# The bias of a pooling mixer: as a one-row product on TensorE, or as a spread row added on VectorE

## The reference

```python
x = layer_norm(ALPHA * x + moe, ln_g[0, 1], ln_b[0, 1])      # end of the first layer
f = pool_mixer(x, pool_w, pool_b, pool_scale)                # (pooled(x) @ w + b) * scale, in 4 groups of 256 columns
x = layer_norm(ALPHA * x + f, ln_g[1, 0], ln_b[1, 0])        # then the router's logits of the second layer
```

## Time and profile before

| | us |
|---|---|
| median of 3 runs | 3657.47 |
| lowest, highest | 3655.7, 3662.36 |
| the profiled execution's own time | 3655.02 |
| its span in the trace | 3653.2 |
| TensorE busy in the span | 3035.5 (83%) |
| VectorE busy in the span | 1163.9 (32%) |
| ScalarE busy in the span | 775.7 (21%) |
| mean granted TensorE clock | 0.919 |

### The profile page before, as it was taken

The page is one execution under the profiler, slowest core; times in us unless marked ns, Lnnn a source line. Parts: engine busy times, 40 slices in busy tenths (PEclk is TensorE's granted clock), DMA queues, the critical chain, the costliest instruction groups (busy, mean ns, idle before and its releaser), DMA issues. The chain is left out here.

```text
span 3653.2 us, 41438 instructions
## 1 busy us (share of the span) xinstructions
PE 3035.5 (83%) x16259; PEld 1793.2 (49%) x16259; DVE 1163.9 (32%) x1986; ACT 775.7 (21%) x1306; POOL 354.6 (10%) x370
## 2 busy tenths in 40 slices
PE   6999879897999999988999997787687577876770
PEld 3455478445888878774555544332222453322220
DVE  1046668223111113321555535211111462111116
ACT  3011222113121212324333311100000331010002
POOL 0000045112000000110000000111110001111102
PEclk9999989898999999999999998899899678998995
DMA  7401000402111114212000022799998437999984
GB/s 264 148 18 34 17 1 1 150 29 87 46 47 51 46 64 143 87 62 90 17 7 6 1 85 113 295 419 419 419 416 335 163 129 293 419 420 420 417 362 197
DMA packets 187340, 615.44 MB, mean 168 GB/s; under 512 B 39241, under 2 KB 101776, under 8 KB 131746
## 3 DMA queue, kind: packets, MB, share of 16 engines
q1 hardware_dynamic: 168738, 579.55, 40.7%
q0 software_dynamic: 18432, 33.60, 2.5%
HBM read 592.08 MB, written 54.53 MB: 177 GB/s over the span
## 5 line engine op out<-in xcount | busy, mean ns | idle before, releaser
L2525 PE MATMUL psum<-moe_ring,hreg 128*32 128x512 f32 x3072 | 387.4, 663 | 144.9 <-DMA moe_ring<-in_moe_w 143.2
L2525 PEld LDWEIGHTS psum<-moe_ring,hreg 128*32 128x32 f32 x3072 | 116.8, 121 | 411.6 <-issue 324.4
L2610 DVE TENSOR_TENSOR ex_hb<-ex_sil,psum 128x256 f32<-128x256 f32 x64 | 26.9, 421 | 639.2 <-ACT ex_sil L2582 639.2
L1084 PE MATMUL psum<-h_hi,gu_hi 128*128 128x512 f32 x704 | 217.7, 391 | 9.2 <-DVE gu_lo L1125 9.2
L1084 PE MATMUL psum<-h_lo,gu_hi 128*128 128x512 f32 x704 | 217.5, 390 | 0.0
L1084 PE MATMUL psum<-h_hi,gu_lo 128*128 128x512 f32 x704 | 217.2, 390 | 0.0
L2557 PE MATMUL psum<-moe_ring,hreg 128*32 128x512 f32 x1728 | 193.7, 601 | 16.2 <-issue 11.3
L501 PE MATMUL psum<-h,pj_w 128*128 128x512 f32 x448 | 194.1, 592 | 0.8 <-ACTq L530 0.8
L2582 ACT ACTIVATE ex_sil<-psum 128x256 f32<-128x256 f32 x64 | 24.5, 383 | 628.9 <-PE psum L2525 628.9
L1084 PEld LDWEIGHTS psum<-h_hi,gu_hi 128*128 128x128 f32 x704 | 132.6, 188 | 36.9 <-issue 9.4
L1084 PEld LDWEIGHTS psum<-h_lo,gu_hi 128*128 128x128 f32 x704 | 132.7, 189 | 27.6
(11 more groups left out here) (498 smaller groups left out, 4819.2 us busy)
## 6 DMA issues: line engine op xcount, KB each, us to landing
moe_ring<-in_moe_w SPq DMA_DIRECT2D x288, 1024.0 KB, 21.1
x<-in_moe_w SPq DMA_DIRECT2D x96, 1024.0 KB, 22.4
draw<-in_w_down SPq DMA_DIRECT2D x44, 512.0 KB, 3.7
XF<-in_w_ada SPq DMA_DIRECT2D x16, 1024.0 KB, 5.8
x<-xrow SPq DMA_DIRECT2D x24, 512.0 KB, 10.4
gu_raw<-in_w_gate SPq DMA_DIRECT2D x22, 512.0 KB, 3.9
gu_raw<-in_w_up SPq DMA_DIRECT2D x22, 512.0 KB, 3.9
mo_dft<-in_dft SPq DMA_DIRECT2D x8, 1024.0 KB, 4.9
```

Of the source, the lines that this page charges most:

```text
L1084: last = pe.matmul(ps[4 * s + 2 * j + h][:, :], w[j][:, k, :], x[:, k, h * 512:(h + 1) * 512], start=k == 0 and n == 0, stop=k == KD - 1 a ...
L2525: last = pe.matmul(ps[i][r, :], xT[i][:, k, r], ring[n % RING][:, j, kk * 512:(kk + 1) * 512], start=k == 0, stop=k == KD - 1)
L2610: dve.tensor_tensor(hb[i][:, :], sil[q % 2][:, :], ps[i][:, DE:2 * DE], ALU.mult).then_inc(hbd, 1)
```

## The change

The rows `c` and `pb` become tiles of 128 equal rows, loaded with a broadcast in the transfer. Their product and sum in `weights()` run on 128 partitions. `residual(t)` gets a drain and an add of `c` behind the product with `ga`. In `mix` the one-row product goes, each group of two products starts its own quarter of PSUM anew, and the wait for `one` goes with the constant.

```diff
-        c, pb, one = sb("c", [1, D]), sb("pb", [1, D]), sb("one", [1, P])
+        c, pb = sb("c", [P, D]), sb("pb", [P, D])
...
-                sp.dma_start(c[:, :], A["ln_b_2"][0, 1:2, :]).then_inc(row_in, 16)
-                sp.dma_start(pb[:, :], A["pool_b_2"]).then_inc(row_in, 16)
+                sp.dma_start(c[:, :], A["ln_b_2"][0, 1:2, :].to_broadcast([P, D])).then_inc(row_in, 16)
+                sp.dma_start(pb[:, :], A["pool_b_2"].to_broadcast([P, D])).then_inc(row_in, 16)
...
-                pool.memset(eps[:, :], LN_EPS)
-                pool.memset(one[:, :], 1.0).then_inc(ones, 1)
+                pool.memset(eps[:, :], LN_EPS).then_inc(ones, 1)
...
-                    dve.tensor_tensor(pb[:, :], pb[:, :], sc[0:1, :], ALU.mult)
+                    dve.tensor_tensor(pb[:, :], pb[:, :], sc[:, :], ALU.mult)
...
                     dve.tensor_tensor(X[:, t, :], n_[t % NN], ga[:, :], ALU.mult).then_inc(scaled, 1)
+                    dve.drain()
+                    dve.tensor_tensor(X[:, t, :], X[:, t, :], c[:, :], ALU.add)
...
-                        pe.wait_ge(ones, 1)
...
-                        pe.matmul(ps[2 + h][:, :], one[:, :], c[:, h * 512:(h + 1) * 512], start=True, stop=False)
                         for g in (2 * h, 2 * h + 1):
                             for k in range(2):
                                 last = pe.matmul(ps[2 + h][:, (g % 2) * 256:(g % 2 + 1) * 256], PM[t % 2][:, 2 * g + k, :], w[:, g, k, :],
-                                                 start=False, stop=g % 2 == 1 and k == 1)
+                                                 start=k == 0, stop=k == 1)
```

## The result

| | before | after |
|---|---|---|
| median, us | 3658.51 (4 runs) | 3635.81 (4 runs) |
| lowest, highest | 3655.7, 3662.36 | 3630.52, 3636.53 |
| the profiled execution's span | 3653.2 | 3628.7 |
| mean granted TensorE clock | 0.919 | 0.921 |

The changed kernel takes 0.9934 of the time of the kernel before, with a 95% interval of 0.9917 to 0.9951. That is faster by 22.7 us at the medians, clearly outside 0.2%. Later sessions agree: medians of 3658.5, 3660.2 and 3658.8 for the kernel before, and of 3635.3 for the changed one in the last of them. The profiled execution of the changed kernel, at 3630.52 us, is the fastest of its four, 5.3 us under their median. So its trace shows a somewhat better case than the median.

The account below looks back on a forecast made before the run. TensorE was taken to bound the stage between the experts. Tile intervals 23.7 us less, last mix 2.1 less, broadcasts 2.5 more: 23.3 less, or 20.3 with 3 us for a remaining clock fall, giving 3637 us; range 3630 to 3647.

Parts of the forecast that it names:

- TensorE sets the pace of the stage: Stage between the experts, about 2844 to 2999 us: TensorE bounds it at 12.14 us a tile; gains reach the end one to one.
- 19.7 us come off TensorE: Sixteen one-row products in the mixes go: 13 at 1.05 us and three at 2.0 us; 2.10 us a steady tile.
- The add costs only what VectorE's pace costs: VectorE, each tile: the new add takes 1.30 us, raising its work to 10.28 us, ahead of TensorE's 10.04.
- a chain over two tiles: One tile followed through the engines to the total of the tile after next: 20.9 us for two tiles, 10.5 a tile.
- The broadcasts cost 2.5 us: Start of the stage, SP's queue: 1.04 MB of spread rows ahead of tile loads 1 to 3 cost 2.5 us in the open.
- The 3.7 us more: Spread-row transfer: the Trainium skill prices 1 MB at 6.15 us, which would make the result 3.7 us later.
- Most falls of the clock go: TensorE in the mixes: 9.9 us went to 1.2 GHz; without the one-row product most falls go, 3 us left in.
- The 3 us that I left in: Allowance, out of 9.9 us, for the clock fall behind tile 1, whose idle 1.27 us ahead of the mix stays.
- (a): TensorE's clock still falls as before: about 9 of the 9.9 us stay, time 3643; chance 0.23.
- (b): VectorE's add lies wholly in the open and the clock falls stay: 6.8 us gained, time 3650.7; chance 0.10.
- (c): No gain: the wait reappears behind the barrier or the first expert transfers, time 3657; chance 0.06.
- (d): TensorE, starved just enough, stays at 1.2 GHz for the whole stage: 18 us slower, 3675; chance 0.05.

Follow-up runs that it names:

- the loop cut: Changed kernel without VectorE's add, ScalarE's second norm of the previous tile moved ahead of the copy of the pooled tile: 3636.10 us, tiles of 9.97 us.
- the swap: ScalarE's second norm of the previous tile put ahead of the pooled tile's copy, against the changed kernel: 3640.16 us with VectorE's add kept, 3636.10 without.
- the one with zeros: Kernel with spread rows and a 128-row product, with ones in the first row and zeros in 127 instead of 1/128 throughout: 3644.05 us.
- the add on top: Kernel before with the two rows spread, one-row product kept, plus the 128x1024 add on VectorE in every tile: 3660.85 us.

## Why the prediction was right, and where its steps were not

The time was 3635.8 for a forecast of 3637, and 22.7 us less at the medians for a forecast of 20.3 less. In the profiled executions it was 24.5 less. Part of this closeness is luck, as the points show:

- **TensorE sets the pace of the stage; what it gains passes on to the end.** Right. 26.4 us less in the stage, 24.5 in the span, with the part behind it within 0.7 us.
- **19.7 us come off TensorE, 2.10 a steady tile.** Too low. The weight load behind the one-row product stood 0.76 us at issue, which I had not seen: 128 rows instead save 0.73 a tile (measured). A full mix took 5.86 us with the one-row products (2923.96 - 2918.10) and takes 3.50 without (2933.24 - 2929.74), so 2.36 us a tile go. TensorE's tile with no waits is 9.97 us, measured with the loop cut, and not the 9.78 which that leaves: 0.2 us came back elsewhere, and I did not pursue it.
- **The add costs only what VectorE's pace costs.** Right in its result: it cost nothing measurable in the kernel before and nothing in the changed one. The pace was right by a wrong path, which is luck. I put 10.28 us down to VectorE, and 10.5 to a chain over two tiles; the average is 10.33 for tiles 2 to 7. VectorE's work is 9.97 (a short operation starts 0.08 us before the end of the long one ahead, as the one at 2916.77 above behind the add that began at 2915.62 and took 1.22, and I had counted such overlap as work), and what holds the tile at 10.28 is a loop of one tile's length through ScalarE's queue that I did not see. The kernel without the add showed it, and the swap cut it; with the add in place the loop is read from the same pace of 10.28, for there the swap brought a new wait.
- **The broadcasts cost 2.5 us.** Right: 2.4 in the kernel with the rows alone and 2.4 in the changed one, by the place of the first mix. The 3.7 us more by the figure of the Trainium skill's "DMA: Bandwidth & Descriptors" did not come about, as the queue was already full and the megabyte cost only its throughput. It was wrong to leave it at that: the rows could have stood behind tile 1's load, and that gains 3.8 us at the medians.
- **Most falls of the clock go.** Right, and bigger than I had it in the first trace. The 3 us that I left in for a fall behind tile 1 were not needed there. And the first interval was 9.16 us where I had 12.0: I had kept the first mix at 1.2 GHz, while in this trace the clock had risen just before it. With 3.0 and 2.8 us those are the two terms that bring my 20.3 to the 26.4 of the stage. Both depend on the execution: the second trace of the changed kernel had 10.66 us and a fall in tile 1's mix. The six intervals behind, 63.1 against 63.0, agree by chance: five took 10.33 on average where I had 10.5, and the first took 11.42 at full clock, with 1.26, 0.73 and 0.49 us of waits on TensorE that I had not counted. The last mix was 2.4 against 2.1. The cause is shown by the pair of kernels that differ in the rows of the product alone, and by the one with zeros: the product of few rows, whether by its rows or by the pause of the weight load behind it. Not shown is that each single fall in the mixes of tiles 2 to 7 is due to it: there were three in the kernel before, three with the add on top, one with the spread rows alone (in tile 7), none with 32 rows. None of the ten traces without such a product had one there.
- **The rivals.** (a) the falls stay: no. (b) the add in the open: no, but one add more, or the swapped queue, brings it there. (c) hidden by what follows: no. (d) starved TensorE at 1.2 GHz: no; it had idle time in each tile and stayed at 1.00 from tile 2's mix to tile 7's, in both traces. Here the rule of the Trainium skill on activity and idleness ("TensorE: Matmul & The Clock Gate", "Part 1: The HAM clock gate") would have led astray if busy time in the profile is taken for activity. With the one-row product the clock fell inside stretches busy 4.00 of 4.00 us, and in the changed kernel it stayed at 1.00 with 0.3 to 0.5 us of idle time a tile.

In sum, against the kernel before, by medians: spread rows +3.8 us, the product at 128 rows -20.6, the product gone -5.1, the add on VectorE -0.8, which is nothing. So 20.6 of the 25.7 us that leaving out the one-row product brought were not its 512 columns, but what its few rows did to the clock and to the weight load behind. The 5.1 us are not the full price of the columns either: two products of 128 rows take 1.82 us of TensorE in a tile, and only 1.13 of it arrives (11.41 to 10.28), since the loop then holds the pace.

## What to carry to other kernels

A bias put into PSUM by a product of one row of ones is not a small product: in this kernel it cost its full 512 columns, delayed the next weight load, and came with a clock held at 1.2 GHz where with products of 128 rows it rose. If VectorE has slack in the tile, spread the row once and add it there; if not, a product of 128 rows of 1/128 on the spread row gave 17 of the 23 us without touching VectorE. Put the spread row's transfer behind the loads that start the pipeline, and before moving work from the bounding engine look for a loop through the queues of the others, which can hold the same pace.

## What the runs showed that I had not expected

- A product of 1 or 32 rows followed by one of 128: half a mix takes 2.98 us, with 128 rows throughout 2.6 us (0.86 to 0.91 and 1.72), in f32 at 2.4 GHz.
- TensorE at 1.2 GHz from 2880 to 2904 while busy 4.00 of 4.00 us in most stretches, with a one-row product in each mix; at 2.4 GHz in the same place with a product of 128 rows, and from 2884 on with 127 of them zeros.
- A VectorE operation on 128x1 elements stretched from 0.16 to 1.25 us beside GpSimd's 2.46 us add.
- One tile pace of 10.28 us with and without 1.3 us of work on VectorE, held by a loop through the queues; VectorE's own work is within 0.3 us of it.
